# Context's gate matrix and keys loaded ahead of the sixteen state stores; query weights in three buffers, the first chunk loaded behind the last context unit

## What is computed

```python
def layer(x, mod, s0, grid_w, p, l):
    shift1, scale1, gate1, shift2, scale2, gate2 = jnp.split(mod, 6, axis=-1)
    h = rmsnorm(x, p['norm_mix'][l]) * (1 + scale1) + shift1
    m, s_fin = mixer(h, s0, grid_w, p, l)      # RWKV-7 scan and Hyena convolution, then @ w_out
    x = x + gate1 * m
    h = rmsnorm(x, p['norm_ffn'][l]) * (1 + scale2) + shift2
    x = x + gate2 * peer(h, p, l)
    return x, s_fin

# in the RWKV part of mixer
    g = jax.nn.sigmoid(h @ p['rwkv_g1'][l]) @ p['rwkv_g2'][l]      # the gate matrix g2
    ...
    out = (yn + bonus.reshape(B, L, D_RWKV)) * g

# in peer
    q = (x @ p['peer_wq'][l]).reshape(T, PEER_HEADS, 2, PEER_HALF)
    s = jnp.einsum('thpd,phkd->thpk', q, p['peer_keys'][l])
    sv, si = lax.top_k(s, PEER_TOPK)
    ...                                        # 128 experts per row: gather, dot, gelu, weighted sum
```

## Time and profile before

| | us |
|---|---|
| median of 3 runs | 2777.74 |
| lowest and highest of them | 2775.55, 2778.43 |
| the profiled execution | 2768.11 |
| its span, first to last instruction | 2766.3 |
| PE busy (matmul) | 2374.0 (86%) |
| DVE busy | 1880.2 (68%) |
| mean granted PE clock | 0.917 |

### The profile page before, as it was taken

How to read it: one execution, slowest core, us unless ns; L and a number is a source line. 1 busy time by engine, 2 the same in 40 slices (tenths; PEclk the granted TensorE clock), 3 DMA queues, 4 the chain that set the end, 5 groups by cost and what they waited for, 6 DMA issues and landing times.

```text
span 2766.3 us, 42661 instructions
## 1 busy us (share of the span) xinstructions
PE 2374.0 (86%) x17458; PEld 1607.1 (58%) x17458; DVE 1880.2 (68%) x3842; ACT 426.7 (15%) x831; POOL 926.9 (34%) x774
## 2 busy tenths in 40 slices
PE   5989978688788788898897289999999999998994
PEld 2545536567677674343444287776776677765552
DVE  1111255345688787675889987887899888867776
ACT  2111213123232221101111121000001000000001
POOL 0000000000023221443634003666665666665671
PEclk8999978789899998998999559999999999999997
DMA  8242130030055543667965206999998999999995
GB/s 292 92 172 72 45 108 23 24 130 2 32 173 176 162 158 118 259 238 251 334 233 178 92 5 241 381 377 380 401 379 324 409 385 387 385 380 409 409 409 205
DMA packets 195293, 638.57 MB, mean 231 GB/s; under 512 B 25158, under 2 KB 27078, under 8 KB 194138
## 3 DMA queue, kind: packets, MB, share of 16 engines
q0 software_dynamic: 110592, 402.70, 39.0%
q1 hardware_dynamic: 84506, 233.13, 22.7%
HBM read 627.11 MB, written 8.65 MB: 230 GB/s over the span
## 4 chain that ended last, share of the span: by engine, by line
PE 62%; DVE 19%; DMA 9%; issue 5%; ACT 2%; POOL 2%; SPq 1%; DVEq 0%; ACTq 0%
PE ps L1044 11%; PE ps L1055 11%; PE ps L584 7%; DMA arena<-in_peer_v,arena 6%; PE ps L1066 6%; PE ps L814 3%; PE ps L971 2%; PE ps L928 2%; PE ps L961 2%; POOL arena L2147 2%; PE ps L586 2%; DVE arena L1821 2%; PE ps L986 1%; DVE arena L1825 1%; DVE arena L1667 1%
## 5 line engine op out<-in xcount | busy, mean ns | idle before, releaser
L1055 PE MATMUL ps<-arena 128*128 128x512 f32 x1024 | 473.9, 606 | 28.7 <-DVE arena L2042 26.7
L1044 PE MATMUL ps<-arena 128*128 128x256 f32 x2048 | 478.6, 387 | 10.7 <-DMA arena<-in_uT 9.7
L2147 POOL DMA_INDIRECT arena<-in_peer_u,arena x256 | 341.3, 1333 | 335.4 <-DVE arena L1788 160.5
L1044 PEld LDWEIGHTS ps<-arena 128*128 128x128 f32 x2048 | 390.6, 194 | 80.3 <-issue 31.8
L2147 POOL DMA_INDIRECT arena<-in_peer_v,arena x256 | 307.6, 1202 | 193.9 <-DVE arena L2001 138.3
L2001 DVE SCALAR_TENSOR_TENSOR arena<-arena 128x1024 f32<-128x1024 f32 x252 | 315.5, 1284 | 73.5 <-DMA arena<-in_peer_v,arena 67.3
L2135 POOL DMA_INDIRECT arena<-in_peer_u,arena x128 | 126.4, 988 | 691.3 <-DVE arena L1788 348.9
L1055 PEld LDWEIGHTS ps<-arena 128*128 128x128 f32 x1024 | 197.2, 194 | 233.7 <-issue 225.6
L1996 DVE SCALAR_TENSOR_TENSOR arena<-arena 128x1024 bf16<-128x1024 f32 x256 | 303.8, 1222 | 39.0 <-DMA arena<-in_peer_u,arena 34.0
L1066 PEld LDWEIGHTS ps<-arena 128*128 128x128 bf16 x3072 | 207.3, 157 | 52.8 <-issue 47.2
L814 PE MATMUL ps<-arena 64*64 64x128 f32 x1920 | 188.1, 285 | 40.9 <-DVE arena L1861 33.3
(11 more groups left out here) (351 smaller groups left out, 3306.7 us busy)
## 6 DMA issues: line engine op xcount, KB each, us to landing
arena<-in_uT SPq DMA_DIRECT2D x128, 512.0 KB
arena<-in_peer_v SPq DMA_DIRECT2D x128, 512.0 KB
arena<-in_w_ada SPq DMA_DIRECT2D x12, 2048.0 KB, 11.5
arena<-in_peer_wq SPq DMA_DIRECT2D x8, 2048.0 KB, 9.3
arena<-in_w_in SPq DMA_DIRECT2D x6, 2048.0 KB, 8.0
arena<-in_w_out SPq DMA_DIRECT2D x4, 2048.0 KB, 7.9
arena<-in_peer_u,arena POOLq DMA_INDIRECT x384
arena<-in_peer_v,arena POOLq DMA_INDIRECT x384
```

Source lines behind the costliest of these rows:

```text
L1044: m = pe.matmul(ps[:, 4 + i % 2, 0:ND], us[i % UB][:, k, :], hTd[:, k, :], start=(k == 0), stop=(k == KD - 1))
L1055: m = pe.matmul(ps[:, 2 * r + c, :], sgel[:, i % SBUFS, P * r:P * r + P], vs[i % VB][:, 512 * c:512 * c + 512], start=(i == 0), stop=(i == ...
L2147: pool.indirect_dma_start(gring[:, n % RING, :], None, a[("peer_u", "peer_v")[e]][0], bass.IndirectOffsetOnAxis(ap=ids[:, t, m:m + 1], axi ...
```

## The change

SP's order is altered, and the query weights get a third buffer:

- the gate matrix is issued at `unit_ok` 2, the keys at `sn_ok`, and chunk 0 of the query weights right behind them, all ahead of the sixteen stores;
- `wc` has a third buffer, at `hv.offset + 3 * DR`, in the region `two`. It lies over `tt2[1]`, `kd2[1]`, `bt2[1]` and half of `lm`, which nobody uses between unit 1 and `begin(2)`; `lm` and `st2[1]` change places so that the latent state stays clear of it;
- chunks 0, 1, 2, 3 of the query weights now lie in buffers 2, 1, 0, 2 (`wq_in`); the semaphore of buffer 2 is `ld_xc`, which already counts the load of `xc`, so the turns are 2, 2, 2, 3 (`wq_turn`);
- chunks 1 and 2 are loaded after the first and second output chunk, chunk 3 after four query products, and the spill of `xc` stands behind it.

```diff
         hc = sc(2, PAIRS, P)
+        lm = two(HEADS, 4, CH)
         st2 = [sc(2, PAIRS, P), two(2, PAIRS, P)]
-        lm = two(HEADS, 4, CH)
...
-        wc = [at(x.offset, KD, 512), at(hT_at + D, KD, 512)]
+        wc = [at(x.offset, KD, 512), at(hT_at + D, KD, 512), at(hv.offset + 3 * DR, KD, 512)]
+        wq_in, wq_turn = (2, 1, 0, 2), (2, 2, 2, 3)
...
-        cw = [sem(f"cw_loaded{i}") for i in range(2)]
+        cw = [sem(f"cw_loaded{i}") for i in range(2)] + [S("ld_xc")]
...
             sp.dma_start(xc, a["x_prompt"][0]).then_inc(S("ld_xc"), 16)
+            sp.wait_ge(S("unit_ok"), 2)
+            sp.dma_start(g2_c, a["rwkv_g2"][0]).then_inc(S("ld_g2"), 16)
             sp.wait_ge(S("sn_ok"), 1)
+            sp.dma_start(keyN_c, a["peer_keys"][0].rearrange("e h k d -> k (e h) d")).then_inc(S("ld_key"), 16)
+            sp.wait_ge(S("ld_xc"), 16)
+            load_wc(2, a["peer_wq"], 0)
             for d in range(2):
                 for h in range(HEADS):
                     i, p = h % 2, h // 2
                     sp.dma_start(new_state[0, 0, d, h], sn[64 * i:64 * i + 64, d, p, 64 * i:64 * i + 64]).then_inc(S("out_state"), 16)
-            sp.wait_ge(S("unit_ok"), 2)
-            sp.dma_start(g2_c, a["rwkv_g2"][0]).then_inc(S("ld_g2"), 16)
-            sp.dma_start(keyN_c, a["peer_keys"][0].rearrange("e h k d -> k (e h) d")).then_inc(S("ld_key"), 16)
             sp.wait_ge(S("oc_mm"), 1)
-            load_wc(1, a["peer_wq"], 0)
+            load_wc(1, a["peer_wq"], 1)
             sp.wait_ge(S("oc_mm"), 2)
-            load_wc(0, a["peer_wq"], 1)
+            load_wc(0, a["peer_wq"], 2)
+            sp.wait_ge(S("q_mm"), 4)
+            load_wc(2, a["peer_wq"], 3)
             sp.wait_ge(S("n2_xn"), 1)
             sp.dma_start(spill[:, 0, :], xc).then_inc(S("xc_out"), 16)
-            sp.wait_ge(S("q_mm"), 4)
-            load_wc(1, a["peer_wq"], 2)
-            sp.wait_ge(S("q_mm"), 8)
-            load_wc(0, a["peer_wq"], 3)
...
-                        pe.wait_ge(cw[(1, 0)[j % 2]], 16 * (2 + j // 2))
+                        pe.wait_ge(cw[wq_in[j]], 16 * wq_turn[j])
...
-                        m = pe.matmul(ps[:, 2 + n % 2, 0:LC], wc[(1, 0)[j % 2]][:, k, P * f:P * f + P], hT_c[:, k, :], start=(k == 0), stop=(k == KD - 1))
+                        m = pe.matmul(ps[:, 2 + n % 2, 0:LC], wc[wq_in[j]][:, k, P * f:P * f + P], hT_c[:, k, :], start=(k == 0), stop=(k == KD - 1))
```

## The result

| | before | after |
|---|---|---|
| median of 5 runs each, us | 2775.55 | 2761.29 |
| lowest and highest | 2772.18, 2778.43 | 2751.98, 2764.77 |
| ratio | | 0.9946, 95% interval 0.9929 to 0.9964 |
| the profiled execution (its span) | 2768.11 (2766.3) | 2751.98 (2750.2) |

The change makes the kernel faster by 0.54% (0.36 to 0.71%), some 15 us. The forecast was 0.41% and 2766.4 us, with 2761.5 to 2771.5 as its range. Some 2 of these 5.1 us are the level it started from (2777.74 as the median of three runs, 2775.55 as that of five), and some 3 are what the medians moved by (14.3 us) beyond the forecast gain of 11.3.

What follows compares the result with a forecast made beforehand. No single bound was seen; in the tail the chain ran through SP's stores and the gate matrix's landing. 9.4 + 1.1 + 0.8 = 11.3 us off the median of 2777.74 gave 2766.4 us, range 2761.5 to 2771.5.

Steps and rivals of the forecast that it cites:

- Gate matrix: Tail, gate product on PE: loaded ahead of the stores, the matrix no longer stalls it; 9.4 us gained.
- Query weights: Query projection: PE's wait for chunk 2 of the query weights goes; 1.1 us gained.
- The top 16: Rival in the query projection: DVE's last top 16 batch becomes the bound, 1.1 us lost, 2767.5 us; chance 0.04.
- Clock: Tail, L723 and L725 on PE: following without a gap, they may run at the raised clock; 0.8 us gained.
- Keys, chunk 0, stores, spill, places: Tail: the other moved loads, stores and spill and the swapped places change nothing, places 0.5 us either way.
- The slower rival: Tail: gate matrix shares DMA engines with keys and chunk 0, gate product 2.9 us later, 2779.5 us; chance 0.03.
- So the end moves with it: Behind the tail: no later stage is set by something older, so the whole 11.3 us reaches the end.
- B: Experiments' theory, stages behind the tail: something in the change shortens them for good, a gain of 15 us or more.
- A: Experiments' theory: the tail's 11.3 us are the whole effect, the rest is scatter of the stages behind it.

Runs made afterwards that it cites:

- e3: Kernel before with the third buffer and swapped places, the stores still ahead of all loads; 0.9990 of the kernel before, tail 85.5 us.
- e4: Kernel before with only lm and st2[1] in each other's place; 0.9992 of the kernel before.
- e6: Changed kernel with the gate matrix issued behind keys and chunk 0, stores still last; one run, 2773.00 us, tail 85.4 us.
- e16: Changed kernel with the eight gate-row spread products moved ahead of unit 1's end, second comparison; 0.9981 of the kernel before.
- e8: Changed kernel plus unused PE transposes, 18 before the scan half's transposes, 7 in each of two pauses before the query projection; 0.9982 of the kernel before.
- gate only: Kernel before with only the gate matrix's load moved ahead of the stores, compared twice; 0.9963 and 0.9961 of the kernel before.
- e7: Changed kernel plus 18 unused PE transposes in the pause before the scan half's transposes; 0.9962 of the kernel before.
- e10: Changed kernel with the eight gate-row spread products moved ahead of unit 1's end, first comparison; 0.9960 of the kernel before.
- e9: Changed kernel plus unused PE transposes, 52 before the scan half's transposes, 18 in each of two pauses before the query projection; 0.9943 of the kernel before.

## Why the prediction was right, and where it failed

- **Gate matrix, 9.4 us.** Right. The idle time is gone, L724 runs behind L716 without a pause, nothing took the stall's place, and alone it gave 10.1 us of tail with its share of the clock.
- **Query weights, 1.1 us.** Right: 1.1 us alone (e3), 1.2 on top of the gate matrix (76.5 to 75.3). The top 16 hid nothing.
- **Clock, 0.8 us.** Right in size. By the chain, L724 and L726 take 2.40 us in place of 2.94, the output projection 16.36 in place of 16.52, the first two query products 5.88 in place of 5.95: 0.54 + 0.16 + 0.07 = 0.77 us.
- **Keys, chunk 0, stores, spill, places: nothing.** Right as far as the tail goes, which came out to 0.1 us: 11.3 forecast, 11.3 measured. For the places, e4 has a tail of 86.7 us; its total bounds them only to between 2 us slower and 7 us faster. Unit 2 begins at 603.59 where the text had said near 603.
- **The slower rival.** It did not happen, and e6 shows that its mechanism is real: with the loads in the other order it costs 10 us. Its price was too high all the same. The prediction added the two landings, 6.8 and 9.3 us, one behind the other. In e6 the gate matrix, last of the three, had landed 13.0 us after the keys were issued, and the tail was 1.2 us shorter than before, where the rival had made it 1.8 us longer.
- **"So the end moves with it", and the range.** This is the step that failed. The sum took the tail's gain to the end unchanged and gave what lies behind it half of the 2.9 us by which three runs had differed. In the first comparison the medians moved by 14.3 us, 3.0 more than the tail. In e16 and e8 the totals came out some 10 and 7 us short of the tail, outside their intervals, so the stages behind it do change with the kernel. In 18 profiles the time from the last query product to the end of the span lies between 2145.6 and 2162.1 us (units, filters, middle and experts added), with mostly the same instructions. The kernel before alone ranges over 7.1 us there, the changed one over 9.5, and the 23 to 29 runs of the kernel before in one comparison over 12 to 18 us. A range of 5 us either way had little room for that. Nor was the level of 2777.74 firm: five runs of the same kernel had 2775.55, and in the later comparisons, on four chips, its median was 2762 to 2764. From 2775.55 the same sum makes 2764.3, and the measured 2761.29 lies only 3 us below it.

**What is open.** The changed kernel gained 13.3 to 15 us in the mean of four comparisons, by medians or by ratios, and its tail has 11.3. Its profiles show no lasting part behind the tail: its four have a mean of 2152.9 us there, the kernel before's four 2156.0, and those two with the old tail or nearly so (e3, e4) 2150.7 and 2146.0. The spread among profiles of one kernel is larger than the 3.1 us, and gate only and e7 gained what their tails had. So for the changed kernel the 2 to 3.6 us beyond the tail may be scatter, but four comparisons that all lie above 0.41% don't look like chance alone, and B is not excluded.

For e8 and e16 scatter is no sufficient account: both gained less than their tails by more than their intervals allow. The kernels with the longest units are e10, e9, e16, e8 and e6, at mean clocks of 0.90 and 0.91. Four of them have tails of 70.4 to 74.9 us, but e6 has 85.4, and e7 with 75.2 has short units, so the length of the tail alone is not what does it. That the stages behind react to when, and in what state of the clock, the tail ends would fit all of this; no run tests it. A is thus shown for the tail and for its parts, and not for the stages behind it.

No kernel of the series beats the changed one by more than can be measured: e9 has 0.9943 against a mean of 0.9946.

## What to carry to other kernels

A queue that issues in the order of the text makes the first reader wait for everything written ahead of it: put loads that somebody waits for ahead of stores that nobody waits for, and among the loads the small one that is needed first ahead of the large ones. Look for it in the chain of waits as a run of issuing entries between two entries of arithmetic.

A term that is read from one stall and its neighbours can be right to a tenth of a microsecond while the total moves by several more. Before a range is given, take two profiles of the same kernel and see how far the stretches differ that the change does not touch. And say beforehand by which figure, the ratio or the medians, an outcome is to be read.

## What the runs showed that I had not expected

- Issues became longer while large loads were under way: chunk 0's own issue took 1.58 us where such an issue took 0.37 otherwise, and the sixteen stores 11.36 us in place of 10.37.
- Plain transposes of the identity kept PE's clock up. In e9 PE did 52 of them in 5.84 us at a granted clock of 1.00, paused 1.1 us, and the output projection began at 1.00 instead of 0.50. The Trainium skill (TensorE: Matmul & The Clock Gate, Part 4: PE-mode transpose) says that the upper clock doesn't engage for transposes; for these, of 32-bit data, the trace shows otherwise, and the measurement decides. The clock rose between 532.4 and 532.8, when PE had just done 6 us of products and transposes, so whether transposes alone would raise it is not shown.
- The same scan units, instruction for instruction, took between 445.3 and 459.9 us, and PE's mean granted clock went from 0.94 to 0.90 with it.
